# Attention heads and output mixing joined into one program block, with semaphores in place of the barrier

## The chip, the cores and the metric

The kernel runs on one core of one Trainium2 chip. The metric is the device time of one execution in microseconds (us). The core has five instruction streams that run beside each other: PE (TensorE, matmuls, with its weight loads shown as PEld), DVE (VectorE), ACT (ScalarE), POOL (GpSimd) and SP (SyncE, which here only issues DMAs). Sixteen DMA engines carry the transfers of two queues that matter here: q1, fed by SP, and q0, fed by POOL.

## The reference, cut to what matters

One layer of an encoder over 1152 tokens (1024 of a prompt and 8 x 16 of samples). The part around the change:

```python
merged = jnp.concatenate([rms_norm(og.reshape(b, t, -1)) for og in outs], axis=-1)   # three head groups
merged = (merged * g_mix_out).astype(h.dtype)
h = h + merged @ w_out                                                              # 1024 x 1024
y = hier_moe(rms_norm(h, norm_ffn).reshape(b * t, D_MODEL), w_rg, b_rg, w_re, b_re, w_eg, w_eu, w_ed)
h = h + y.reshape(b, t, D_MODEL).astype(h.dtype)
```

`outs` are the outputs of 16 attention heads. The router inside `hier_moe` takes the top group of 4 and two experts in it.

## The kernel before, in words

The program has four stages, each a block of its own: projection, heads, mixing and experts (`moe`). A block ends with a barrier over all five engines.

**Heads** (`heads`, lines 773 to 1254) goes through units of work, each one query tile of a pair of heads, software-pipelined over the engines: at step x, PE transposes the probabilities of unit x (`turn`, L1034), makes the scores of unit x + 2, transposes back the output of unit x - 2 (`back`, L1021) and multiplies with the values of unit x - 1 (`values`, L1058, or L745 and L749 for a sample unit). ACT copies and moves (`move`, L1119), DVE scans, weighs (`weigh`, L1176), copies and writes the rows (`write`). The last units are stick-breaking ones of a single head, and the very last, NU - 1, is a sample unit. Beside them the first steps of mixing are already done: `group_scale` and `norm_heads` normalise token tile 0 into `m2`, and PE transposes it (L1079) after the last values.

SP's list of heads ends with the loads for mixing: the gain `g_mix_out` (L948), the two halves of `w_out`, 2 MB each in rows of 2 KB (L950), the gain `norm_ffn` (L951), the router's weights (L952, rows of 80 bytes), its bias (L953), a column form of the gain (L954), and then a wait for all of them, `mix_loaded`, ahead of the barrier.

**Mixing** (`mixing`, lines 1280 to 1566) multiplies each of the nine token tiles with `w_out` in float32 made of parts: `split` rounds one of 8 slices (k) of a half of `w_out` on ACT (L1448), `lower_weights` subtracts that on DVE (L1509), and PE makes three matmuls of 512 columns for each k (L1374). The same is done with the transposed tile: `copy_first` (L1443) or `copies` (L1439) on ACT, and `lower` on DVE (L1518). For tile n, PE does `mix(n, 0)`, `mix(n, 1)`, transposes (L1356) and the router's logits (L1394). DVE adds the residual (`residual`, L1491), which needs both halves and the x rows that SP loaded (L1335). That sets `h_ready`, and `mix(n + 1)` waits for it.

POOL makes small tables of counts at the start of mixing, a zero tile in the memory of `z`, and issues 32 DMAs of 416 KB (L1561) that write zeros to the DRAM table `grouped`, 13 MB in all. Then it clears the semaphores of the former stages.

Memory of heads that is given back (probabilities, transposed probabilities, biases) is taken again by mixing's tiles.

Of the kernel before, what the change touches and what calls it, by code (L numbers as in the profile page):

```python
# [25 lines left out]
P = 128  # L26
# [746 lines left out]
def heads(nc, c, a, dram, merged, released, early, late, mixw):  # L773
# [6 lines left out]
    name = "heads_"  # L780
    with ExitStack() as ctx:
        sb = lambda n, s, d=F32: ctx.enter_context(nc.sbuf_tensor(name + n, s, d))
        ps = lambda n, s: ctx.enter_context(nc.psum_tensor(name + n, s, F32))
# [75 lines left out]
        mix_loaded = sem("mix_loaded")  # L859
# [24 lines left out]
        def copied(e, G):  # L884

            e.wait_ge(copied_dve if by_dve[G] else copied_act, sum(1 for F in range(G + 1) if by_dve[F] == by_dve[G]))

        with nc.Block() as block:
            @block.sync
            def _(sp):  # L890
# [58 lines left out]
                for i in two:  # L949
                    sp.dma_start(mixw["w_out"][i], wv[:, :, 512 * i:512 * i + 512]).then_inc(mix_loaded, 16)  # L950
                sp.dma_start(mixw["gff"], a["norm_ffn"].partition_broadcast(P)).then_inc(mix_loaded, 16)  # L951
                sp.dma_start(mixw["w_r"][:, :, :], a["w_router"].rearrange("(k p) n -> p k n", p=P)).then_inc(mix_loaded, 16)  # L952
                sp.dma_start(mixw["b_r"][:, :], a["b_router"].partition_broadcast(P)).then_inc(mix_loaded, 16)  # L953
                sp.dma_start(mixw["gcol"][:, :], a["norm_ffn_cols"]).then_inc(mix_loaded, 16)  # L954
                sp.wait_ge(mix_loaded, 16 * 6)

            @block.gpsimd
            def _(pool):
                for g, (h0, nh) in enumerate(pairs):
                    if not band(g):  # L960
                        continue
                    u = g % 2
                    pool.wait_ge(bias_loaded[u], expected(bias_n, g))
                    pool.memset(bias[u][HD:P, 0:nh, SEQ - PAST:SEQ - PAST + HD], NEG)
                    pool.memset(bias[u][0:HD, 0:nh, SEQ + HD:TOK], NEG).then_inc(bias_ready, 1)

            @block.tensor
            def _(pe):
# [94 lines left out]
                for x in range(NU + 2):  # L1063
# [11 lines left out]
                pe.wait_ge(opened, stuck[NU])  # L1075
                pe.wait_ge(mixw["m_normed"], 1)
                for half in two:
                    for j in range(4 * half, 4 * half + 4):
                        mm = pe.transpose(score[:, 0, P * j:P * j + P], mixw["m2"][:, P * j:P * j + P], ident[:, :])  # L1079
                    mm.then_inc(mixw["m_turned"], 1)  # L1080

            @block.scalar
            def _(act):
# [37 lines left out]
                for x in range(NU + 1):  # L1121
                    mine = [G for G in range(piece0[x], piece0[x + 1]) if not by_dve[G]] if x < NU else []
# [9 lines left out]
                    if x + 3 == NU:  # L1132
                        act.preload_act_table_set("natural_log_exp_and_others")
                    if x:
                        move(x - 1)
                    if x + 3 == NU:
                        act.wait_ge(written, NU - 4)
                        group_scale(act, c, merged[:, 0, :], mixw["m2"], mixw["sm"][:, 0, :], mixw["act_chain"], 0)
                        act.sem_inc(mixw["m_scale"], 1)

            @block.vector
            def _(dve):
# [86 lines left out]
                for x in range(NU + 2):  # L1229
# [21 lines left out]
                    if x == NU - 2:  # L1251
                        dve.wait_ge(mixw["gmo_loaded"], 16)
                        dve.wait_ge(mixw["m_scale"], 1)
                        norm_heads(dve, merged[:, 0, :], mixw["sm"][:, 0, :], mixw["gmo"], mixw["m2"]).then_inc(mixw["m_normed"], 1)

# [24 lines left out]
def mixing(nc, c, a, dram, merged, h, logits, released, mixw, x_stored, wg_raw, g_ple, counts, gate_loaded):  # L1280


    with ExitStack() as ctx:
        sb = lambda n, s, d=F32: ctx.enter_context(nc.sbuf_tensor("mix_" + n, s, d))
        ps = lambda n, s: ctx.enter_context(nc.psum_tensor("mix_" + n, s, F32))
        sem = lambda n: ctx.enter_context(nc.semaphore("mix_" + n))
        two = range(2)
        w_out, w_low, w_r, b_r, gmo, gff, gcol = (mixw[n] for n in ("w_out", "w_low", "w_r", "b_r", "gmo", "gff", "gcol"))
        w_high = [sb(f"w_high{i}", [P, KD, 512], F32R) for i in two]
        xr = sb("xr", [P, 2, D])  # L1290
        xn = sb("xn", [P, 2, D])
        rest_m2 = sb("m2", [P, D])
        m2 = [mixw["m2"]] + [rest_m2[:, :]] * (NT - 1)
        pair_mT = [sb(f"mT{u}", [P, KD, P], F32R) for u in two]
        pair_low = [sb(f"mT_low{u}", [P, KD, P], F32R) for u in two]
        mT = [mixw["mT"]] + [pair_mT[n % 2][:, :, :] for n in range(1, NT)]
        mT_low = [mixw["mT_low"]] + [pair_low[n % 2][:, :, :] for n in range(1, NT)]
        hT = sb("hT", [P, KD, P])
        sq = mixw["spare"][:, 0:D]
        sm = mixw["sm"]  # L1300
        sh = sb("sh", [P, 2])
        zeros = mixw["spare"][0:ROWS, D:D + D // 4]
        tm, tx = (mixw["score"][:, i, :].rearrange("p (u n) -> p u n", u=2) for i in two)
        om = ps("om", [P, 2, 512])
        lg = ps("lg", [P, 512])

        x_loaded = [sem(f"x_loaded{u}") for u in two]
# [1097 lines left out]
```

## Time and profile before

| what | us |
|---|---|
| median of 3 runs | 1264.49 |
| lowest and highest of the 3 | 1264.01, 1267.06 |
| the profiled execution's own time | 1266.51 |
| span of the profile (first to last instruction) | 1264.9 |
| PE busy | 1209.3 |
| heads end, mixing begins | about 665 to 670 |
| mixing ends | about 809 |

The span lies 1.6 us under the profiled execution's own time, which in turn lies 2 us over the median. Positions in the text are microseconds from the span's start.

### The profile page before, as it was taken

The page shows a single profiled execution, that of the slowest core. Times are in us where ns is not written, and L with a number is a line of the kernel's source. Part 1 is how long each engine was busy: PE and PEld are TensorE (multiplying, and loading weights), DVE is VectorE, ACT ScalarE, POOL GpSimd, SP SyncE. Part 2 cuts the span into 40 slices and gives each one's busy share as a digit, 9 for nine tenths or more (in the row PEclk, how much of TensorE's full clock was granted, in tenths as well). Part 3 has the DMA queues.
Part 4 walks back from the last instruction along what each step waited for, and adds up shares of the span by engine and source line. Part 5 has one row for each costly group of instructions (what it writes and reads, how often), then busy time and mean ns, then how long its engine had stood idle before and what let it go on. Part 6 is the DMA issues. An engine that isn't in the chain of part 4 may idle for free. (4 is left out here: it accounts for less than half of the span.)

```text
span 1264.9 us, 19690 instructions
## 1 busy us (share of the span) xinstructions
PE 1209.3 (96%) x7464; PEld 955.3 (76%) x7464; DVE 607.9 (48%) x1095; ACT 503.1 (40%) x1073; POOL 128.9 (10%) x195
## 2 busy tenths in 40 slices
PE   6999999999999999988997999799999999999998
PEld 4878888888766666655666888569999999986886
DVE  4734674310145555579985333563333343344553
ACT  5713222221255556568765344433222222213221
POOL 2000000000000000000008000031111111004321
PEclk9999999999999999989998999789999999999999
DMA  8623444514186556463458982297878888755531
GB/s 295 219 67 95 144 118 133 154 59 155 39 278 214 189 199 200 120 223 125 126 214 213 259 280 94 83 306 267 278 245 269 276 258 259 251 164 170 184 117 50
DMA packets 101980, 233.65 MB, mean 185 GB/s; under 512 B 23191, under 2 KB 50850, under 8 KB 95757
## 3 DMA queue, kind: packets, MB, share of 16 engines
q1 hardware_dynamic: 79212, 166.50, 39.2%
q0 software_dynamic: 16160, 53.50, 14.5%
q10 hardware_dynamic: 6528, 12.58, 3.8%
q8 instruction: 51, 0.84, 0.3%
q14 instruction: 29, 0.23, 0.1%
HBM read 174.70 MB, written 59.81 MB: 185 GB/s over the span
## 5 line engine op out<-in xcount | busy, mean ns | idle before, releaser
L1868 PE MATMUL moe_gu<-moe_xT,moe_room 128*128 128x208 f32 x1024 | 188.4, 343 | 0.6 <-ACT moe_xT L1996 0.6
L438 PE MATMUL zp<-w_low,x_high 128*128 128x512 f32 x432 | 175.3, 406 | 10.9 <-DVE w_low L586 8.9
L1868 PEld LDWEIGHTS moe_gu<-moe_xT,moe_room 128*128 128x128 f32 x1024 | 182.0, 192 | 2.5 <-ACT moe_xT L1996 0.9
L438 PE MATMUL zp<-w_high,x_low 128*128 128x512 f32 x432 | 171.4, 397 | 0.0
L438 PE MATMUL zp<-w_high,x_high 128*128 128x512 f32 x432 | 171.4, 397 | 0.0
L521 ACT ACTIVATE z<-zp,ssx 128x512 f32<-128x512 f32 x54 | 37.1, 687 | 203.9 <-PE zp L438 203.9
L438 PEld LDWEIGHTS zp<-w_low,x_high 128*128 128x128 f32 x432 | 81.7, 189 | 31.5 <-DVE x_low L581 11.1
L1034 PE MATMUL heads_turn<-ident,heads_prob 128*128 128x128 f32 x596 | 90.9, 283 | 7.3 <-ACT heads_probT L1112 5.5
L1087 ACT ACTIVATE heads_prob<-heads_prob,least 128x640 f32<-128x640 f32 (+7 forms) x95 | 69.2, 728 | 70.1 <-DVE least L1161 70.1
L438 PEld LDWEIGHTS zp<-w_high,x_high 128*128 128x128 f32 x432 | 81.7, 189 | 19.8
L438 PEld LDWEIGHTS zp<-w_high,x_low 128*128 128x128 f32 x432 | 81.9, 190 | 17.8
L2098 DVE COPY moe_y<-moe_yp 104x512 f32<-104x512 f32 x60 | 41.4, 691 | 106.6 <-PE moe_yp L1880 106.6
L1943 PE MATMUL moe_gu<-moe_wg_high,moe_wd_high 128*128 128x512 f32 x288 | 90.1, 393 | 0.0
L1034 PEld LDWEIGHTS heads_turn<-ident,heads_prob 128*128 128x128 f32 x596 | 65.3, 142 | 24.2 <-issue 11.8
L1112 ACT ACTIVATE heads_probT<-heads_turn 128x512 f32<-128x512 f32 (+1 forms) x131 | 68.5, 542 | 16.0 <-PE heads_turn L1034 15.5
L598 DVE TENSOR_TENSOR sq<-z 128x512 f32<-128x512 f32 (+1 forms) x36 | 18.9, 526 | 93.4 <-ACT z L521 93.4
L1943 PEld LDWEIGHTS moe_gu<-moe_wg_high,moe_wd_high 128*128 128x128 f32 x288 | 54.1, 188 | 12.5
L1188 DVE COPY heads_probT<-heads_turn 128x512 f32<-128x512 f32 (+3 forms) x51 | 31.1, 615 | 57.7 <-PE heads_turn L1034 57.5
L2004 ACT ACTIVATE moe_sig<-moe_gu 128x416 f32<-128x416 f32 x16 | 8.3, 517 | 125.7 <-PE moe_gu L1868 125.7
L1374 PE MATMUL mix_om<-w_out_low,mix_mT 128*128 128x512 f32 x128 | 51.8, 405 | 1.7 <-DVE mix_mT_low L1518 1.7
L586 DVE SCALAR_TENSOR_TENSOR w_low<-h,gmix,w_high 128x512 fp32r<-128x512 f32 x48 | 35.4, 745 | 36.7 <-ACT w_high L493 36.7
L1996 ACT ACTIVATE moe_xT<-moe_tp 128x416 f32<-128x416 f32 x64 | 29.7, 515 | 57.3 <-PE moe_tp L1862 57.3
(354 smaller groups left out, 2141.0 us busy)
## 6 DMA issues: line engine op xcount, KB each, us to landing
moe_room<-in_w_gu SPq DMA_DIRECT2D x16, 2048.0 KB, 10.2
moe_room<-in_w_ed POOLq DMA_DIRECT2D x16, 1024.0 KB, 11.5
scratch_grouped<-z POOLq DMA_DIRECT2D x32, 416.0 KB, 26.4
scratch_grouped<-moe_y SPq DMA_DIRECT2D x15, 832.0 KB
h<-in_w_in ACTq DMA_DIRECT2D x24, 512.0 KB, 5.0
scratch_qkT<-ring SPq DMA_DIRECT2D x36, 256.0 KB, 2.6
heads_ckT<-in_cache_kT SPq DMA_DIRECT2D x9, 1024.0 KB, 5.0
heads_cv<-in_cache_v SPq DMA_DIRECT2D x9, 1024.0 KB, 5.0
```

What stands on the lines that cost most here:

```text
L438: mm = pe.matmul(zp[:, U % 3, :], xs[:, k, n * P:n * P + P], ws[g % 2][:, k, :], start=(k == 0 and i == 0), stop=(k == KD - 1 and i == 2))
L521: act.activation(z[:, U % ZS, :], zp[:, U % 3, :], ACT.Copy, scale=ssx[:, 0, n:n + 1]).then_inc(group_taken, 1)
L586: dve.scalar_tensor_tensor(out=w_low[g % 2][:, k, :], in0=w_raw[:, k, :], scalar=gmix[:, k:k + 1], in1=w_high[g % 2][:, k, :].bitcast(F32) ...
L1034: mm = pe.transpose(tp[:, G % 2, P * x:P * x + P], weights_of(U, e)[:, P * b:P * b + P], ident[:, :])
L1087: act.activation(p, p, ACT.Exp, bias=least[:, U % 4, e:e + 1], scale=-1.0, accum_out=total[:, U % 4, e:e + 1]).then_inc(expd, 1)
L1112: act.activation(probT[:, U % 2, i:i + n, :].rearrange("p j n -> p (j n)"), tp[:, G % 2, 0:P * n], ACT.Copy)\
L1188: dve.tensor_copy(probT[:, U % 2, i:i + n, :].rearrange("p j n -> p (j n)"), tp[:, G % 2, 0:P * n])\
L1374: mm = pe.matmul(om[:, half, :], ms[n][:, k, :], ws[half][:, k, :], start=(k == 0 and i == 0), stop=(k == KD - 1 and i == 2))
L1868: mm = pe.matmul(gu[:, u, side, BS * f:BS * f + BS], wgu[u][:, k, DE * side + P * f:DE * side + P * f + P], xT[u][:, k, :], start=(k == 0 ...
L1943: mm = pe.matmul(gu[:, u, half, :], xs[u][:, k, :], ws[half][:, k, :], start=(k == 0 and i == 0), stop=(k == KD - 1 and i == 2))
L1996: act.activation(xT[u][:, 2 * g:2 * g + 2, :].rearrange("p j n -> p (j n)"), tp[:, g % 2, 0:2 * BS], ACT.Copy).then_inc(copied, 1)
L2098: dve.tensor_copy(to[:, t, 512 * half:512 * half + 512], yp[0:ROWS, half, :]).then_inc(y_taken, 1)
```

## The change

Mixing is no longer a block. Its five engine programs are functions (`sync`, `tensor`, `scalar_first`, `scalar`, `vector`, `gpsimd`) that heads calls at the end of its own, so that one block holds both and the barrier between them and the wait for `mix_loaded` are gone. The memory is planned as before (heads' tiles are released in the plan ahead of mixing's), and waits on counts stand where the barrier stood.

- ACT splits slices 0 to 2 of the first half before its last `move`, slice 3 after it; slices 4 to 7 wait until all values are summed; the second half waits for its own load.
- DVE lowers slices as they come, and does the last `write` and the scaling of the router's weights only after `norm_merged(1)`, ahead of `residual(0)`. The scaling waits for the four small loads.
- PE transposes tile 0 ahead of the last values.
- SP loads the x rows after the last `turn` of heads.
- POOL makes its tables once the last band bias is ready, and zeroes and issues the 32 DMAs once the last `weigh` is done. It clears the semaphores after `h_ready` is 1.

```diff
-                for i in two:
-                    sp.dma_start(mixw["w_out"][i], wv[:, :, 512 * i:512 * i + 512]).then_inc(mix_loaded, 16)
-                sp.dma_start(mixw["gff"], a["norm_ffn"].partition_broadcast(P)).then_inc(mix_loaded, 16)
-                sp.dma_start(mixw["w_r"][:, :, :], a["w_router"].rearrange("(k p) n -> p k n", p=P)).then_inc(mix_loaded, 16)
-                sp.dma_start(mixw["b_r"][:, :], a["b_router"].partition_broadcast(P)).then_inc(mix_loaded, 16)
-                sp.dma_start(mixw["gcol"][:, :], a["norm_ffn_cols"]).then_inc(mix_loaded, 16)
-                sp.wait_ge(mix_loaded, 16 * 6)
+                    sp.dma_start(mixw["w_out"][i], wv[:, :, 512 * i:512 * i + 512]).then_inc(mixw["w_out_loaded"][i], 16)
+                sp.dma_start(mixw["gff"], a["norm_ffn"].partition_broadcast(P)).then_inc(mixw["small_loaded"], 16)
+                sp.dma_start(mixw["w_r"][:, :, :], a["w_router"].rearrange("(k p) n -> p k n", p=P)).then_inc(mixw["small_loaded"], 16)
...
+                mix["sync"](sp)
...
+                pool.wait_ge(bias_ready, sum(1 for g in range(len(pairs)) if band(g)))
+                mix["gpsimd"](pool)
...
+                    if x == NU:
+                        turn_first_mixed()
                     if 0 <= x - 1 < NU:
                         values(x - 1)
...
+                    if x == NU - 1:
+                        mix["scalar_first"](act)
                     if x:
                         move(x - 1)
...
+        sp.wait_ge(*mixw["heads_turned"])
                 load(0)
                 load(1)
...
+    def scalar_first(act):
+        act.wait_ge(mixw["w_out_loaded"][0], 16)
+        split(act, 0, range(0, 3))
...
-                act.wait_ge(m_turned, 2)
+        split(act, 0, (3,))
                 copy_first(0)
-                split(0, range(0, 2))
                 copy_first(1)
-                split(0, range(2, KD))
-                split(1)
+        act.wait_ge(*mixw["heads_summed"])
+        split(act, 0, range(4, KD))
+        act.wait_ge(mixw["w_out_loaded"][1], 16)
+        split(act, 1)
...
+        def scale_router():
+            dve.wait_ge(mixw["small_loaded"], 16 * 4)
...
+        pool.wait_ge(*mixw["heads_weighed"])
                 pool.memset(zeros[:, :], 0.0).then_inc(zero_made, 1)
...
+        pool.wait_ge(h_ready, 1)
                 for s in released:
                     pool.sem_clear(s)
```

PE at the end of heads, before (`heads_out` is the output of the values, `score<-ident,w_gate_raw` the transposes of tile 0, `mix_om` the output of mixing):

```order
L1021 MATMUL heads_out<-ident,ring 128x128 [waits heads_moved]
L745 MATMUL heads_out<-ring,heads_probT 128x128 [waits heads_copied_dve,heads_cv_loaded,heads_written]
L749 MATMUL heads_out<-heads_cv0,heads_probT 32x128 x16
L1079 MATMUL score<-ident,w_gate_raw 128x128 [waits m_normed,heads_opened]
L1079 MATMUL score<-ident,w_gate_raw 128x128 x7
L888 UNCONDITIONAL_BRANCH
L1349 UNCONDITIONAL_BRANCH [waits barrier_Pool_Activation_PE_DVE_SP_release]
L1374 MATMUL mix_om<-w_out_low0,w_high 128x512 [waits mix_w_lowered,mix_m_lowered]
```

and now:

```order
L1027 MATMUL heads_out<-ident,ring 128x128 [waits heads_moved]
L1074 MATMUL score<-ident,w_gate_raw 128x128 [waits m_normed,heads_opened]
L1074 MATMUL score<-ident,w_gate_raw 128x128 x7
L745 MATMUL heads_out<-ring,heads_probT 128x128 [waits heads_copied_dve,heads_cv_loaded,heads_written]
L749 MATMUL heads_out<-heads_cv0,heads_probT 32x128 x16
L1385 MATMUL mix_om<-w_out_low0,w_high 128x512 [waits mix_w_lowered,mix_m_lowered]
```

The transposes moved ahead of the last values, and the branch and the barrier between them and the first mixing matmul are gone.

DVE from the last slices of the weights to the first residual, now (`w_out_low0` and `w_out_low1` are the lowered halves, `w_gate_raw` and `mix_m2` the normalised tiles):

```order
L1524 TENSOR_TENSOR w_out_low0<-past1,mix_w_high0 128x512 [waits mix_w_split] x5
L1524 TENSOR_TENSOR w_out_low1<-w_out1,mix_w_high1 128x512 [waits mix_w_split] x8
L768 SCALAR_TENSOR_TENSOR mix_m2<-h,merged_scales,heads_kT1 128x384 [waits m_turned,m_scale]
L768 SCALAR_TENSOR_TENSOR mix_m2<-h,merged_scales,heads_kT1 128x320 x2
L1223 TENSOR_TENSOR ring<-heads_out,parity 128x64 [waits heads_summed]
L1224 TENSOR_TENSOR ring<-heads_out,parity 128x64
L1225 TENSOR_TENSOR h<-ring 128x64 [waits heads_pick_chain]
L1529 TENSOR_TENSOR w_router<-w_router,norm_ffn_cols 128x160 [waits mix_small_loaded]
L1506 TENSOR_TENSOR h<-mix_om,mix_xr 128x1024 [waits mix_mixed,mix_x_loaded0]
```

The last write of heads and the router's scaling stand between the second tile's normalisation and the first residual, and the scaling carries the wait for the small loads.

POOL, before:

```order
L965 MEMSET heads_bias1 64x64
L888 UNCONDITIONAL_BRANCH
L1539 UNCONDITIONAL_BRANCH [waits barrier_Pool_Activation_PE_DVE_SP_gather]
L1541 IOTA mix_desc_i 128x4
...
L1557 MEMSET z 104x256
L1561 DMA scratch_grouped<-z 416x1x256 [waits mix_zero_made]
L1561 DMA scratch_grouped<-z 416x1x256 x31
```

and now:

```order
L969 MEMSET heads_bias1 64x64
L1562 IOTA mix_desc_i 128x4 [waits heads_bias_ready]
...
L1579 MEMSET z 104x256 [waits heads_weighed]
L1583 DMA scratch_grouped<-z 416x1x256 [waits mix_zero_made]
L1583 DMA scratch_grouped<-z 416x1x256 x31
```

The tables and the zeroing follow counts of heads and no longer the barrier.

## Rows read from the trace of the kernel before

**Rows 1.** The page: busy us, share and instructions of each engine.

```profile
PE 1209.3 (96%) x7464; PEld 955.3 (76%) x7464; DVE 607.9 (48%) x1095; ACT 503.1 (40%) x1073; POOL 128.9 (10%) x195
```

**Rows 2.** Stretches: length, busy PE, PEld, DVE, ACT, POOL, clock, DMA share, GB/s.

```profile
660.00:665.00 5.00, 4.53 (x65) 3.33 (x63) 3.30 (x12) 0.34 (x2) 0.00 (x0) 1.00 1.06 399
672.00:674.00 2.00, 2.00 (x6) 1.55 (x5) 2.00 (x4) 2.00 (x5) 2.00 (x3) 0.50 0.36 90
698.00:712.00 14.00, 14.00 (x76) 11.78 (x75) 5.43 (x8) 6.03 (x17) 0.00 (x0) 1.00 0.98 247
```

**Rows 3.** PE in time: start, us, line, count, idle before and its releaser.

```profile
663.85 1.09 PE L1079 MATMUL score<-ident,w_gate_raw 128*128 128x128 f32 x8
670.22 0.77 PE L1374 MATMUL mix_om<-w_out_low,w_high 128*128 128x512 f32 x1 [5.28 <-DVE w_out_low L1509]
...
683.63 1.04 PE L1356 MATMUL score<-ident,mix_m 128*128 128x128 f32 x8
686.38 0.50 PE L1374 MATMUL mix_om<-w_out_low,mix_mT 128*128 128x512 f32 x1 [1.71 <-DVE mix_mT_low L1518]
...
697.58 1.03 PE L1356 MATMUL score<-ident,h 128*128 128x128 f32 x8
```

**Rows 4.** ACT and DVE in time, from the last weigh to the first residual.

```profile
661.71 0.28 ACT L1119 ACTIVATE ring<-heads_out 128x128 f32<-128x128 f32 x1 [1.65 <-PE heads_out L1058]
673.17 4.27 ACT L1448 ACTIVATE mix_w_high<-w_out 128x512 fp32r<-128x512 f32 x8
...
656.30 0.82 DVE L1176 TENSOR_TENSOR heads_prob<-heads_prob,z 128x639 f32<-128x639 f32 x1
674.86 4.89 DVE L1509 TENSOR_TENSOR w_out_low<-w_out,mix_w_high 128x512 fp32r<-128x512 f32 x8
680.11 1.54 DVE L768 SCALAR_TENSOR_TENSOR mix_m<-h,merged_scales,heads_kT 128x384 f32<-128x384 f32 x3
683.90 1.23 DVE L1491 TENSOR_TENSOR h<-mix_om,mix_xr 128x1024 f32<-128x1024 f32 x1 [2.25 <-PE mix_om L1374]
```

**Rows 5.** SP and POOL in time: when each DMA is issued.

```profile
648.25 1.28 SPq L950 DMA_DIRECT2D w_out<-in_w_out  x1
662.79 0.43 SPq L954 DMA_DIRECT2D norm_ffn_cols<-in_norm_ffn_cols  x1
...
671.94 24.05 POOL L1561 DMA_DIRECT2D scratch_grouped<-z  x31 [0.31 <-POOL z L1557]
...
856.64 0.76 POOL L1818 DMA_DIRECT2D moe_room<-in_w_ed  x1 [10.82 <-DMA scratch_ple<-moe_late_ple]
```

**Rows 6.** DMA issues: count, KB, us to landing, one window for each.

```profile
past<-in_w_out SPq DMA_DIRECT2D x1, 2048.0 KB, 12.0
w_out<-in_w_out SPq DMA_DIRECT2D x1, 2048.0 KB, 16.6
norm_ffn_cols<-in_norm_ffn_cols SPq DMA_DIRECT2D x1, 4.0 KB, 4.8
mix_xr<-in_x SPq DMA_DIRECT2D x1, 512.0 KB, 3.6
mix_xr<-in_x SPq DMA_DIRECT2D x1, 512.0 KB, 15.7
w_gate_raw<-in_w_ple_gate SPq DMA_DIRECT2D x1, 2048.0 KB, 33.1
```

**Rows 7.** DMA queues: packets, MB, share; 725 to 730, then 860 to 863.

```profile
q0 software_dynamic: 284, 0.82, 56.4%
q1 hardware_dynamic: 396, 0.86, 44.2%
...
q1 hardware_dynamic: 66, 1.08, 84.8%
q0 software_dynamic: 39, 0.16, 12.9%
```

**Rows 8.** q1 in 665 to 666, alone on the engines.

```profile
q1 hardware_dynamic: 831, 0.07, 63.0%
```

More of the change, by code:

```diff
@@ L886, in copied @@
             e.wait_ge(copied_dve if by_dve[G] else copied_act, sum(1 for F in range(G + 1) if by_dve[F] == by_dve[G]))
+        memory.close()
+        mixw["heads_turned"], mixw["heads_summed"], mixw["heads_weighed"] = (turned, piece0[NU]), (summed, NU), (weighed, stuck[NU])
+        mix = follow(ctx)
         with nc.Block() as block:
@@ L1061, in values, with turn_first_mixed @@
                     mm.then_inc(summed, 1)
-                for x in range(NU + 2):
+                def turn_first_mixed():
+                    pe.wait_ge(opened, stuck[NU])
+                    pe.wait_ge(mixw["m_normed"], 1)
+                    for half in two:
+                        for j in range(4 * half, 4 * half + 4):
+                            mm = pe.transpose(score[:, 0, P * j:P * j + P], mixw["m2"][:, P * j:P * j + P], ident[:, :])
+                        mm.then_inc(mixw["m_turned"], 1)
+                for x in range(NU + 1):
                     if x < NU:
@@ L1071, in _ @@
                         turn(x, True)
+                    if x == NU:
+                        turn_first_mixed()
                     if 0 <= x - 1 < NU:
                         values(x - 1)
[L1075 to L1080, printed above, removed]
+                mix["tensor"](pe)
             @block.scalar
@@ L1119, in move @@
                         act.activation(oT[:, U % 2, :], op[:, U % 2, 0:P], ACT.Copy).then_inc(moved, 1)
-                for x in range(NU + 1):
-                    mine = [G for G in range(piece0[x], piece0[x + 1]) if not by_dve[G]] if x < NU else []
+                for x in range(NU):
+                    mine = [G for G in range(piece0[x], piece0[x + 1]) if not by_dve[G]]
                     while mine and mine[0] < piece0[x] + 2:
@@ L1227, in write @@
                     ins.then_inc(written, 1)
-                for x in range(NU + 2):
+                for x in range(NU + 1):
                     mine = [G for G in range(piece0[x], piece0[x + 1]) if by_dve[G]] if x < NU else []
@@ L1254, in _ @@
                         norm_heads(dve, merged[:, 0, :], mixw["sm"][:, 0, :], mixw["gmo"], mixw["m2"]).then_inc(mixw["m_normed"], 1)
+                mix["vector"](dve, lambda: write(NU - 1))
 def shift(n, u, m, d):
@@ new lines, in tensor, with split @@
+        n = NT - 1
+        mix(n, 0).then_inc(half_mixed, 1)
+        turn_rows(n - 1)
+        mix(n, 1, range(0, KD // 2))
+        route(n - 1)
+        turn_last(0)
+        mix(n, 1, range(KD // 2, KD)).then_inc(mixed, 1)
+        turn_last(1)
+        route(n)
+    def split(act, i, ks=range(KD)):
+        for k in ks:
+            act.activation(w_high[i][:, k, :], w_out[i][:, k, :], ACT.Copy).then_inc(w_split, 1)
+    def scalar_first(act):
+        act.wait_ge(mixw["w_out_loaded"][0], 16)
+        split(act, 0, range(0, 3))
@@ L2334, in program @@
             mixw |= {n: sem(n) for n in ("gmo_loaded", "act_chain", "m_scale", "m_normed", "m_turned")}
-            heads(nc, c, a, dram, merged, released, early, late, mixw)
+            mixw |= {"w_out_loaded": [sem(f"w_out_loaded{i}") for i in range(2)], "small_loaded": sem("mix_small_loaded")}
             x_stored = [sem(f"x_rows_stored{u}") for u in range(2)]
             gate_loaded = sem("gate_loaded")
-            mixing(nc, c, a, dram, merged, h, logits, released, mixw, x_stored, wg_raw, g_ple, counts, gate_loaded)
+            follow = lambda ctx: mixing(nc, ctx, c, a, dram, merged, h, logits, released, mixw, x_stored, wg_raw, g_ple, counts, gate_loaded)
+            heads(nc, c, a, dram, merged, released, early, late, mixw, follow)
             attention.close()
```

507 lines of the change are left out of this document (249 added, 258 removed).

## The prediction, made before the changed kernel was run

> **What bounds the kernel now.** I began with the page: PE is busy for 1209.3 of 1264.9 us [rows 1], so a change pays only where it gives PE something to do while it stands idle or slow. Then the table by stretches [rows 2]. In the steady part of mixing PE is busy for all of 14.00 us out of 14.00, at granted clock 1.00; no other engine is near that, so from the second tile on mixing runs at PE's pace, and whatever shifts its start shifts everything after it. The exception is the seam: about 665 to 670 PE does nothing [rows 3], and from 672 to 674 it is busy at a clock of 0.50, the lower of its two levels (1.2 GHz), after that idle stretch [rows 2]. PE in order of time gives the edges [rows 3]: the transposes of tile 0 end at 664.94, the first mixing matmul starts at 670.22 after 5.28 us idle, mix(0) ends about 683.63, and mix(1) starts at 686.38. This last number is my milestone: the kernel after gains or loses what mix(1) moves.
>
> Why the gap is 5.3 us: SP waits for the small loads ahead of the barrier. The last of them is issued at 662.79 and lands 4.8 us later, at 667.6 [rows 5, 6]; then come barrier, first copy, first lowering. The loads of w_out themselves are in time: issued at about 647.8 and 648.25, they land at 659.8 and 664.85 [rows 5, 6].
>
> **The change, compute alone.** No load is counted yet.
> - ACT does three splits ahead of its last move. Eight splits take 4.27 us [rows 4], so three take about 1.6. The first half lands at 659.8 and the move comes at 661.71 after 1.65 us idle [rows 4]: they just fit, cost 0 (up to 1 us if that load slips).
> - PE: the transposes (1.09 us) change places with the last values; a tie. DVE has lowered its first slice and the first half tile by about 664.9, so mix(0) starts at about 665.0 and not at 670.2.
> - mix(0) took 13.4 us, from 670.22 to 683.63 [rows 3]. With the clock kept it takes 16 slices at the steady pace: mix(1) is the same 48 matmuls with nothing to wait for, from 686.38 to 697.58, 11.2 us [rows 3], so mix(0) would end at 676.2. The cold clock thus cost about 2.2 us.
> - DVE then is late: the 16 lowerings, at 4.89 us for eight [rows 4], end at about 674.2; normalising tile 1 (1.54) waits for ACT's scales and ends at 676.2; the write that moved behind it and the router's scaling add 1.0, the residual 1.23, the lowering of tile 1 another 1.3. mix(1) starts at 679.8.
> - Sum: 679.8 - 686.38 = -6.6 us. The residual would start at 677.2 instead of 683.90 [rows 4].
> - Tables on POOL, made early: nothing waits for them, 0. Clearing semaphores: POOL has over 100 us for it, 0.
>
> **What the change sets loose.** This decides it. POOL's 32 zeroing DMAs (13 MB) no longer start at 671.94 but once the last weigh is done. That ends at 656.30 + 0.82 = 657.12 [rows 4]; with the zero tile made the first goes out at about 657.6, the next ones every 24.05 / 31 = 0.78 us [rows 5]. Before, all loads for mixing and the first two of x had landed by then. Now this stream meets on the 16 engines, already full (DMA share 1.06 at 399 GB/s [rows 2]), all that q1 still owes: most of the second half of w_out, the 512 KB of norm_ffn, some 1280 packets of 80 bytes and less, and the x rows. And two waits stand on these: ACT's second split on w_out's second half, DVE's residual(0) on the small loads (through the router's scaling) and on x. Behind that wait DVE's whole list is queued, and mix(1) needs both its residual and its lowering.
>
> How q1 fares beside q0. In 725 to 730, with the same zeroing deep in its queue, q1 moved 0.86 MB in 396 packets and q0 0.82 MB in 284 [rows 7]: q1 has 172 GB/s against about 400 alone. Single loads show worse, since a load waits for its slowest engine: x rows that take 3.6 us on a free machine took 15.7, and a 2 MB load of the same rows of 2 KB as w_out took 33.1 [rows 6]. A kinder row: where q1 has the backlog and q0 comes later (860 to 863), q0 got only 39 packets against 66 [rows 7], and its load had been issued at 856.64, over 3 us earlier [rows 5]; so the flood may bite only from about 661 on.
> - Second half of w_out: from 661, some 1.55 MB are left. At 172 GB/s that is 9 us, landing at 670; at the pace of the 2 MB load behind its x rows (33.1 less 15.7 gives 17.4 us for 2 MB) 13.5 us, landing at 674.5. I take 674, the nearer shape.
> - norm_ffn: 0.5 MB at 172 GB/s, 3 us: 677.
> - The small packets: alone, 831 packets went by in 1 us [rows 8], so 1.5 us for 1280. If each takes a turn against a packet of q0, at the 396 packets in 5 us of 725 to 730, they take 16 us. Nothing in the trace shows small packets in the flood. I take 8, the middle, and keep 1.5 and 16: 685.
> - x rows: 0.5 MB, 3 us, and 1 us to be reported: 689.
>
> The Trainium skill (DMA: Bandwidth & Descriptors, Queues, rings and completion order) says that each DMA engine goes round the queues that have work for it packet by packet, whatever queue came first. The near equal counts of the two queues in 725 to 730 agree with it roughly, and it speaks against starting the zeroing early; taken strictly it gives the 16 us for the small packets.
>
> **Sum.** The residual starts at 689 and not at 683.9: +5.1. PE, done with mix(0) by about 683, is idle for some 8 us before mix(1); an idle of 5.28 brought it to 0.50 and cost 2.2 us, so I add 2.3 for the longer one. Together +7.4 us. I set it against the median (the profiled run lies 2 us higher, the same shift applies to it): 1264.5 + 7.4 = 1271.9, said as 1272. After mix(1) PE's pace rules again; zeroing ends some us earlier, which nobody waits for.
>
> **The rivals.**
> 1. The loads are in time, faster. If q1's backlog goes first and small packets are nearly free, everything for residual(0) lands by 680: then the compute chain rules, -6.6, or 1258; with w_out at 670 and residual(0) at 680, about -4. For: the late start of q0 at 860. Against: 172 GB/s in 725 to 730, over many us. It would need the flood to cost less than 13 us over the 667.6 at which the last small load landed before.
> 2. Each small packet takes a turn, slower by much: the small loads end at 677 + 16 = 693, x at 697, and with the cold clock +15.4, or 1280; with w_out's half as slow as the whole 2 MB load (648.25 + 33.1 = 681, 7 us later) +22, or 1287. It decides from the point where the small loads land after 684.
> 3. Break-even: residual(0) between 680 and 688, the gap filled and the same time lost again on x. 1261 to 1268. PE then idles at 676 to 686 instead of at 665 to 670.
> 4. The change does not do what it says (the early splits delay ACT's last move by a us or more, because w_out's first half slips as well): 1 us at most, inside the range of the others.
>
> **How the numbers follow.** Faster than 1260.7 (rival 1): 0.26. Between 1260.7 and 1268.3 (rival 3, with the lower edge of the forecast): 0.24. My forecast's neighbourhood, 1268.3 to 1278: 0.28. Rival 2: 0.22. A difference of 0.3%, 3.8 us, is about the least that a measurement of this kernel can tell from no change. So faster 0.26, same 0.24, slower 0.50. The range that leaves about 2 in 10 out is 1258 to 1285.
>
> **What would show it.** The gap of PE at 665 should be gone, mix(0) should start near 665 at clock 1.00: both are sure. Then POOL's zeroing at 657.6, and the landing of w_out's second half (now 664.85): 674 for my case, under 668 for rival 1, over 680 for rival 2. DVE's router scaling waiting for a DMA, and residual(0) for a DMA on x; PE idle for 5 us or more ahead of mix(1), and its clock at 0.50 after. If residual(0) instead waits for PE only, I am wrong in the term of the flood. If mixing's later tiles take more than 14 us each, I missed contention of the x loads further on, which nothing waits for now: PE is busy 14.00 of 14.00 us there.

## The result, and the profile after

The changed kernel takes 1283.08 us (median of 4 runs, 1280.26 to 1288.64), the kernel before 1265.44 us (median of 4 runs): ratio 1.0141, 95% interval 1.0120 to 1.0162, or 17.6 us slower. The prediction said 1272, 7 us slower, with a range of 1258 to 1285. The direction holds, and so does the mechanism in kind (DVE waits for small loads that meet the early zeroing); the size is more than twice the forecast, because the small loads were priced at 8 us and took 20.8. The profiled execution of the changed kernel took 1280.26 us, with a span of 1278.3 us, 13.4 us over the span of before.

PE at the seam, kernel after; columns: start us, us, engine, line, operation, names, shapes, count, and in brackets the idle time before it and what ended it. These answer to [rows 3].

```profile
661.24 1.04 PE L1074 MATMUL score<-ident,w_gate_raw 128*128 128x128 f32 x8
662.43 1.08 PE L749 MATMUL heads_out<-heads_cv,heads_probT 128*32 128x128 f32 x32
663.65 0.50 PE L1385 MATMUL mix_om<-w_out_low,w_high 128*128 128x512 f32 x1
...
673.08 0.47 PE L1385 MATMUL mix_om<-w_out_low,w_high 128*128 128x512 f32 x1 [3.56 <-DVE w_out_low L1524]
680.29 1.04 PE L1367 MATMUL score<-ident,mix_m 128*128 128x128 f32 x8
698.95 0.80 PE L1385 MATMUL mix_om<-w_out_low,mix_mT 128*128 128x512 f32 x1 [17.62 <-DVE mix_mT_low L1538]
712.68 1.04 PE L1367 MATMUL score<-ident,h 128*128 128x128 f32 x8
```

The gap of 5.28 us at the end of heads is gone: the first mixing matmul follows the last values at once, at 663.65. But PE stops for 3.56 us in the middle of mix(0), and then for 17.62 us before mix(1), the milestone of the prediction: it starts at 698.95 and not at 686.38. The page of after has the same wait as the only large one of that line, out of 128 matmuls:

```profile
L1385 PE MATMUL mix_om<-w_out_low,mix_mT 128*128 128x512 f32 x128 | 52.8, 413 | 17.6 <-DVE mix_mT_low L1538 17.6
```

Who made PE wait stands in the time lines of ACT and DVE (answering to [rows 4]):

```profile
660.74 0.28 ACT L1129 ACTIVATE ring<-heads_out 128x128 f32<-128x128 f32 x1
671.58 4.29 ACT L1428 ACTIVATE mix_w_high<-w_out 128x512 fp32r<-128x512 f32 x8 [5.80 <-DMA w_out<-in_w_out]
...
678.53 1.54 DVE L768 SCALAR_TENSOR_TENSOR mix_m<-h,merged_scales,heads_kT 128x384 f32<-128x384 f32 x3 [1.38 <-ACTq L1438]
694.15 0.33 DVE L1529 TENSOR_TENSOR w_router<-w_router,norm_ffn_cols 128x160 f32<-128x160 f32 x1 [13.56 <-DMA norm_ffn_cols<-in_norm_ffn_cols]
696.47 1.23 DVE L1506 TENSOR_TENSOR h<-mix_om,mix_xr 128x1024 f32<-128x1024 f32 x1 [1.99 <-DMA mix_xr<-in_x]
```

Three waits for a DMA, one behind the other: ACT for w_out's second half (5.80), DVE's scaling of the router's weights for the last small load (13.56), and DVE's residual for x (1.99). DVE had done the moved write by 680.6, and did nothing from then to 694.15.

The issuing engines, in time (answering to [rows 5]):

```profile
656.84 24.05 POOL L1583 DMA_DIRECT2D scratch_grouped<-z  x31 [0.31 <-POOL z L1579]
...
647.27 1.46 SPq L954 DMA_DIRECT2D w_out<-in_w_out  x1
648.77 6.75 SPq L955 DMA_DIRECT2D heads_v<-in_norm_ffn  x1
655.56 0.52 SPq L956 DMA_DIRECT2D w_router<-in_w_router  x1
656.13 13.72 SPq L957 DMA_DIRECT2D b_router<-in_b_router  x1
669.89 3.63 SPq L958 DMA_DIRECT2D norm_ffn_cols<-in_norm_ffn_cols  x1
```

The landings (answering to [rows 6]): count, KB, us from issue to landing. `heads_v` is the memory that norm_ffn is loaded to.

```profile
w_out<-in_w_out SPq DMA_DIRECT2D x1, 2048.0 KB, 24.3
heads_v<-in_norm_ffn SPq DMA_DIRECT2D x1, 512.0 KB, 24.5
w_router<-in_w_router SPq DMA_DIRECT2D x1, 80.0 KB, 25.3
b_router<-in_b_router SPq DMA_DIRECT2D x1, 10.0 KB, 28.7
norm_ffn_cols<-in_norm_ffn_cols SPq DMA_DIRECT2D x1, 4.0 KB, 24.2
```

So w_out's second half lands at 647.27 + 24.3 = 671.6, norm_ffn at 673.3, the router's weights at 680.9, its bias at 684.8 and the last 4 KB at 694.1. The last four loads count on one semaphore, 16 steps each, and the profile gives the 16th, 32nd, 48th and 64th step to them in the order of issue: only 694.1, the last of all, is a landing beyond doubt. (Before, all six loads shared `mix_loaded`, so the same holds for the single landings that the prediction read there.) The queues in 670 to 680 (packets, MB, share of the 16 engines) show how:

```profile
q0 software_dynamic: 831, 2.44, 94.9%
q1 hardware_dynamic: 800, 0.10, 6.7%
```

Nearly equal numbers of packets, 831 and 800, but the 831 carry 2.44 MB and the 800 carry 0.10 MB. By the sizes in the trace, 594 of the 831 are packets of 4 KB (the others of 16 and 4 bytes), and 752 of the 800 are packets of 80 bytes. In [rows 8] 831 such packets of q1 went by in one microsecond, alone; beside the zeroing they need more than ten.

From here to the end the extra time stays: mixing ends at 824.43 instead of 809.23, and the experts give back 1.8 us.

**A yardstick for all that follows.** Heads end earlier or later by up to 6 us in these traces, with how often the granted clock of PE drops to 0.50 ahead of their end: never in e1 (last weigh at 653.78), in four stretches in e3 (659.72). So I cut each trace into three: the seam, from the start of the last weigh on DVE to the first matmul of mix(1) (before: 656.30 to 686.38); mixing, from there to SP's first load of the experts (809.23); the rest, from there to the end of the span. us:

| kernel | seam | mixing | rest | median of its runs, ratio to before (95%) |
|---|---|---|---|---|
| before | 30.1 | 122.9 | 455.7 | |
| after | 43.6 | 125.5 | 453.9 | 1283.1, 1.0141 (1.0120 to 1.0162) |
| e1 late zeroing | 22.6 | 123.8 | 455.8 | 1265.9, 1.0005 (0.9979 to 1.0031) |
| e7 the same, second look | 22.3 | 133.8 | 456.0 | 1271.3, one run |
| e2 small loads first | 26.3 | 125.4 | 453.5 | 1263.8, 0.9999 (0.9977 to 1.0021) |
| e8 the same, second look | 24.3 | 124.3 | 455.8 | 1263.1, one run |
| e3 router packed | 33.4 | 124.3 | 455.9 | 1269.8, 1.0039 (1.0021 to 1.0057) |
| e4 before, zeroing early | 89.7 | 122.7 | 452.6 | 1324.4, 1.0482 (1.0444 to 1.0520) |
| e5 late zeroing, small first | 22.8 | 126.0 | 456.2 | 1263.8, 0.9986 (0.9956 to 1.0016) |
| e6 before, small first | 30.6 | 122.9 | 455.6 | 1265.4, 0.9994 (0.9975 to 1.0014) |
| e10 eight zeroing DMAs early | 27.7 | 124.5 | 456.0 | 1266.9, 1.0019 (0.9999 to 1.0038) |
| e12 late zeroing, gate loads later | 22.4 | 123.0 | 453.0 | 1259.6, 0.9953 (0.9938 to 0.9968) |
| e9 late and paced zeroing | 22.4 | 122.8 | 452.8 | 1259.1, 0.9959 (0.9939 to 0.9978) |
| e11 paced, small first | 22.3 | 122.7 | 455.1 | 1256.0, 0.9932 (0.9908 to 0.9956) |

The mixing of after holds 2.5 us of cold clock (mix(1) takes 13.73 us for its 48 matmuls instead of 11.2). The last column differs by up to 3.6 us between kernels that are alike in the experts (452.6 in e4, 456.2 in e5); no experiment asks why, so no difference there is put down to an edit. All experiments compute the whole reference.

### The profile page after: what moved, and what is told of

The parts are those of the page before. It is cut to its first block and busy times, and to the rows that moved or that the text cites. A ratio compares the mean times of both kernels' runs of the same rounds, so it can differ in the third digit from the quotient of the medians.

```text
span 1278.3 us, 19677 instructions
## 1 busy us (share of the span) xinstructions
PE 1208.2 (95%) x7464; PEld 955.1 (75%) x7464; DVE 607.9 (48%) x1095; ACT 503.1 (39%) x1073; POOL 128.4 (10%) x195
## 5 line engine op out<-in xcount | busy, mean ns | idle before, releaser
L438 PEld LDWEIGHTS zp<-w_high,x_low 128*128 128x128 f32 x432 | 81.8, 189 | 17.6
L1385 PE MATMUL mix_om<-w_out_low,mix_mT 128*128 128x512 f32 x128 | 52.8, 413 | 17.6 <-DVE mix_mT_low L1538 17.6
```

The costliest lines, as they stand in the source:

```text
L438: mm = pe.matmul(zp[:, U % 3, :], xs[:, k, n * P:n * P + P], ws[g % 2][:, k, :], start=(k == 0 and i == 0), stop=(k == KD - 1 and i == 2))
L1385: mm = pe.matmul(om[:, half, :], ms[n][:, k, :], ws[half][:, k, :], start=(k == 0 and i == 0), stop=(k == KD - 1 and i == 2))
```

## The experiments

### Is it the early zeroing? e1 and e4

e1 is the changed kernel with the zeroing alone put back behind the first residual:

```diff
         pool.wait_ge(*mixw["heads_weighed"])
+        pool.wait_ge(h_ready, 1)
         pool.memset(zeros[:, :], 0.0).then_inc(zero_made, 1)
...
-        pool.wait_ge(h_ready, 1)
         for s in released:
```

> The changed kernel with one wait added: POOL makes the zero tile and issues its 32 zeroing DMAs only once the first residual is done. All else of the change stays. Theory A (the early zeroing is the whole loss): all loads land as before (last small one by about 668), PE has no gap at 665 and starts mix(1) at about 680 instead of 686.4, so 6.6 us under the kernel before, about 1259 us. Rival B (the loss comes from another part: SP's order, the moved write and scaling, the missing barrier): the router's scaling still waits for a DMA until 690 or so, and the time stays at 1275 to 1283 us. In between (1264 to 1270) both would have a share.

At the seam theory A is right to a microsecond: PE has no gap and starts mix(1) at 676.36, the seam takes 22.6 us, 7.5 under before and 21.0 under after. DVE reaches the residual at 673.89 without a wait for a DMA, and all 64 steps of the small loads' semaphore come between 662.2 and 665.2, where after they run from 666.5 to 694.1. PE and DVE in its trace:

```profile
676.36 0.50 PE L1385 MATMUL mix_om<-w_out_low,mix_mT 128*128 128x512 f32 x1 [1.71 <-DVE mix_mT_low L1538]
...
673.89 1.23 DVE L1506 TENSOR_TENSOR h<-mix_om,mix_xr 128x1024 f32<-128x1024 f32 x1 [0.19 <-PE mix_om L1385]
```

So the early zeroing is the cause of the loss at the seam. But the median, 1265.9, is that of the kernel before. The ten executions scatter from 1258.0 to 1273.9, and the trace was of the fastest. Something else takes the gain back; e7 below looks for it.

e4 is the opposite: the kernel before with the early zeroing alone. The memset and the 32 DMAs stand on POOL behind the last weigh, inside heads:

```diff
+                pool.wait_ge(weighed, stuck[NU])
+                pool.memset(zeros, 0.0).then_inc(mixw["zero_made"], 1)
...
+                for j in range(4 * LEAST_PAIRS, 4 * PAIRS):
+                    pool.dma_start(dram["grouped"]...
```

> The kernel before with one part of the change alone: POOL zeroes and issues its 32 DMAs inside heads, once the last weigh is done; barrier and wait for all six loads stay. Theory A (the early zeroing is the cause): the small loads land near 694 instead of 667.6, and the barrier, which waits for them, opens 26 us later; with a longer cold stretch of PE that makes 24 to 29 us over the kernel before, 1289 to 1294 us. Rival B (the zeroing costs little by itself; the other parts of the change lose the time): at most 5 us over, under 1271 us.

It is slower by 60 us, over twice what I expected. The small loads land as I said (bias at 687, last 4 KB at 692), but the barrier does not open then. POOL and PE in its trace:

```profile
660.01 24.05 POOL L972 DMA_DIRECT2D scratch_grouped<-z  x31 [0.31 <-POOL z L968]
725.93 0.75 POOL L972 DMA_DIRECT2D scratch_grouped<-z  x1 [41.87 <-issue]
...
732.53 0.76 PE L1381 MATMUL mix_om<-w_out_low,w_high 128*128 128x512 f32 x1 [65.40 <-DVE w_out_low L1516]
```

POOL issues 31 of the 32 DMAs in 24 us and is then held for 41.87 us before it can issue the last, and the barrier needs POOL. The same stands in the traces of before (65.95 us, to 761.94) and after (56.61, to 737.49), where nobody waits for POOL at that time. So the early zeroing alone costs time, as theory A says, but e4 loses it by another wait than the one in its theory, and its 60 us say nothing of the price of the small loads. What they show is that the early zeroing needs the barrier gone: with it kept, the loss is 60 us and not 18.

### Packets or bytes? e2, e3 and e10

e2 keeps the early zeroing and moves the three small loads (router's weights, bias, gain columns) to the head of SP's list of heads:

```diff
+                sp.dma_start(mixw["w_r"][:, :, :], a["w_router"].rearrange("(k p) n -> p k n", p=P)).then_inc(mixw["small_loaded"], 16)
+                sp.dma_start(mixw["b_r"][:, :], a["b_router"].partition_broadcast(P)).then_inc(mixw["small_loaded"], 16)
+                sp.dma_start(mixw["gcol"][:, :], a["norm_ffn_cols"]).then_inc(mixw["small_loaded"], 16)
                 for g in range(len(pairs)):
                     load_past(g)
...
```

> The changed kernel, with the early zeroing, but with the router's weights, its bias and the gain columns (1280 packets of 80 bytes and less, 0.1 MB) issued at the head of SP's list of heads, hundreds of us earlier. Turn theory (each small packet takes a turn against a 4 KB packet of the zeroing): their 20.8 us between norm_ffn's landing (673.3) and their own (694.1) go away, x rows land by about 678, DVE reaches the first residual at about 681 and mix(1) starts at about 683 to 684: 2 to 3 us under the kernel before, or 1261 to 1264 us. Byte theory (the flood takes bandwidth, the count of packets doesn't matter): 0.1 MB less to move changes under 1 us, x rows still land near 695 and the time stays within 3 us of the changed kernel, 1280 to 1283 us.

The turn theory holds: 0.1 MB less in the queue takes 17.3 us off the seam (26.3 against 43.6) and 19 us off the median (1263.8). DVE's residual starts at 681.07, without a wait for a DMA, and mix(1) at 683.53:

```profile
681.07 1.22 DVE L1506 TENSOR_TENSOR h<-mix_om,mix_xr 128x1024 f32<-128x1024 f32 x1
```

The byte theory had this at 1280 or more and falls. A second look at the same kernel (e8) gives 24.3 us at the seam, a little under the 25 to 28 I expected; its two traces have the clock under 1.00 in heads between 540 and 600 us, as those of before and after have too.

> The same kernel as the one with the small loads first, for a second look: does the seam (from the last weigh to the first matmul of mix(1), 26.3 us in the first trace against 30.1 in the kernel before) hold, and where do its executions differ (1260.5 to 1270.1)? I expect the seam at 25 to 28 us, and the difference in heads, at stretches with a granted clock under 1.00 between 540 and 600 us.

e3 leaves the order and shrinks the packets: the router's weights lie in DRAM as they will lie in memory, so that the load is 128 packets of 640 bytes.

```diff
-                sp.dma_start(mixw["w_r"][:, :, :], a["w_router"].rearrange("(k p) n -> p k n", p=P)).then_inc(mixw["small_loaded"], 16)
+                sp.dma_start(mixw["w_r"][:, :, :], a["w_router"]).then_inc(mixw["small_loaded"], 16)
...
-"w_router": np.concatenate([...], axis=1),
+"w_router": np.concatenate([...], axis=1).reshape(KD, P, NG + NE).transpose(1, 0, 2),
```

> The changed kernel, with the early zeroing and the old order of loads, but with the router's weights laid out so that their load is 128 packets of 640 bytes instead of 1024 of 80 bytes: same bytes, an eighth of the packets (384 small ones in all instead of 1280). Turn theory: the small loads end at about 678 to 682 instead of 694.1, the first residual starts at 682 to 685, mix(1) at 685 to 688, and the time is 1265 to 1269 us. Byte theory: nothing changes, 1280 to 1283 us. If SP's long issue (13.7 us for the bias load) is what counts and it doesn't depend on the packets queued ahead, it also stays above 1275.

Faster by 13 us than after (1269.8), at the seam by 10.2. That is between the two theories and nearer to the turn theory, though just outside its 1265 to 1269. The router's weights now pass quickly (issued at 660.84, landed 15.7 us later, 2.3 us behind norm_ffn instead of 7.6). But the last small load still lands 13.9 us behind norm_ffn, with 384 packets, where 1280 took 20.8. The number of packets is not all of it. The rows of its queues in 675 to 685 (packets, MB, share) say what the rest is,

```profile
q0 software_dynamic: 662, 1.94, 74.6%
q1 hardware_dynamic: 559, 0.88, 23.2%
```

and DVE in time:

```profile
688.08 0.33 DVE L1529 TENSOR_TENSOR w_router<-w_router,norm_ffn_cols 128x160 f32<-128x160 f32 x1 [2.60 <-DMA norm_ffn_cols<-in_norm_ffn_cols]
```

In 675 to 685 q1 moved 0.88 MB, nearly all of it x rows, which were issued behind the small loads; and yet the small loads were not complete before 688. My reading: a queue is spread over the 16 engines, each engine goes on to x when its own share is done, and a load counts as landed when the slowest engine has done its share. From the two traces, (20.8 - 13.9) us for 896 packets, I estimate 8 ns per packet, and some 11 us that don't depend on their number. The estimate is weak, since e3 also freed SP, which issued the last small load at 662.05 and not at 669.89.

The trace of after bears the reading out. The steps of the shared semaphore come one by one, the last sixteen of them between 685.4 and 694.1; in e1, without the flood, the last sixteen come within 1.5 us (663.7 to 665.2). And of the 1152 packets of 80 bytes, which began at 666.1, 785 pass in 669 to 679, 79 a us; from 681 on only 109 are left, and these need till 691, while the x rows behind them already move. So the turns set the pace of the bulk, and a tail of slow shares sets the landing. Why some shares are slow stays open.

e10 leaves packets and order and shortens the flood: 8 DMAs go out early, then 4 after each residual.

```diff
         for j in range(4 * LEAST_PAIRS, 4 * PAIRS):
+            late = j - 4 * LEAST_PAIRS - 8
+            if late >= 0 and late % 4 == 0:
+                pool.wait_ge(h_ready, late // 4 + 1)
             pool.dma_start(dram["grouped"]...
```

> The changed kernel, but only the first 8 of the 32 zeroing DMAs (3.4 MB) go out early; the others follow 4 after each residual. Turn theory: the small packets only take turns while q0 has work; at the 240 GB/s that q0 had in 670 to 680, 3.4 MB are gone by about 677, then the rest of the small packets passes at 831 in a us, so they end at 678 to 681 and not at 694; the seam takes 25 to 28 us (43.6 in the changed kernel, 30.1 before), the time is 1259 to 1263 us. If any early zeroing costs the same (a start-up effect, SP's blocked issue), the seam stays above 35 us and the time above 1270.

The mechanism is met: the small loads end at 679.9 (expected 678 to 681), the seam takes 27.7 us (25 to 28). The rival of SP's blocked issue falls too, since SP is held nearly as long as in after:

```profile
655.89 11.33 SPq L957 DMA_DIRECT2D b_router<-in_b_router  x1
```

The median is not met: 1266.9 against 1259 to 1263. The trace has 2.4 us less at the seam than before and 1.6 more in mixing, where mix(1) begins after an idle stretch of 5.42 us with matmuls of 0.80 us and not of 0.50; the rest of the difference lies in executions that I have no trace of.

### Were the small loads the gap of before? e6

The kernel before with the small loads first, barrier kept.

> The kernel before with one edit alone: router's weights, bias and gain columns loaded at the head of SP's list of heads; barrier kept, which now waits for w_out and norm_ffn only. The last small load landed at 667.6 and held the barrier; w_out was there at 664.85, the transposes of PE end at 664.94. Theory (the barrier's wait for the small loads was 2 to 3 us of the gap of 5.28): the gap becomes about 2.5 to 3 us, and mix(1) comes 2 to 3 us earlier, 1261 to 1262.5 us. Rival (the barrier itself and the first copy and lowering are the gap): under 0.5 us of change.

The rival has the number, 1265.4 us with a gap of 5.59 us, but not the cause: the barrier still waits for a load. Without the small loads it is norm_ffn, issued at 651.77 and landed 18.1 us later, at 669.9; the first copy starts at 670.31. So some 3.0 us of the gap (PE is idle from 666.91) are a wait for a DMA, and 2.6 are barrier, copy and lowering. On engines with no second queue the 1280 packets had cost nothing that counts. My sentence that the barrier waits for the small loads was right as a row, and wrong as a price.

### Where does late zeroing lose its gain? e7, e5, e9, e12, e11

e7 is e1 again, for a second trace.

> The same kernel as the one with the late zeroing, for a second look at its trace: its first profile (1257.96 us) lay at the low end of its ten executions (1258.0 to 1273.9), and this asks where the others lose. If the clock of TensorE drops in stretches of heads, the last weigh starts later than 653.8 and the seam still takes 22 to 23 us; if the seam itself varies, it takes more than 25 us; if mixing or the experts vary, their stretches (112.6 us from the end of mix(1) to the end of mixing, 455.8 from there to the end) get longer.

It caught a long one, 1271.3 us: seam 22.3 and rest 456.0, as in e1, but mixing 133.8 instead of 123.8. (The other 3.5 us between the two traces lie in heads.) The stretches (length, busy PE, PEld, DVE, ACT, POOL, then clock, DMA share, GB/s):

```profile
750.00:757.00 7.00, 1.24 (x10) 0.90 (x8) 2.21 (x4) 1.09 (x2) 0.00 (x0) 0.78 0.78 245
757.00:772.00 15.00, 14.41 (x55) 12.54 (x56) 6.03 (x10) 5.16 (x15) 0.00 (x0) 0.65 0.61 218
```

PE and DVE in time:

```profile
757.59 1.97 PE L1367 MATMUL score<-ident,mix_m 128*128 128x128 f32 x8 [6.35 <-DVE mix_m L768]
...
754.79 1.28 DVE L1491 SCALAR_TENSOR_TENSOR mix_xn<-h,mix_sh,heads_v 128x1024 f32<-128x1024 f32 x1 [15.38 <-DMA scratch_x_rows<-mix_xn]
```

DVE waits 15.38 us until the rows of tile 2 are stored, since tile 4's take their place; behind that wait stand the normalising of the next tile and so PE, idle for 6.35 us and then at a clock of 0.65. SP issued that store at 711.35, right behind a 2 MB load of gate weights (707.61, landed 40.0 us later); the store itself took 43.3 us. In the faster trace of e1 DVE's waits for such stores took 11.1 us in three pieces, in before 3.2 in one. Before had this collision too, with just enough slack; late zeroing lays its 13 MB fully over tiles 1 to 6 and uses it up.

e5 is late zeroing with the small loads first; its expectation was written before e7's trace was known:

> Both mends together: the changed kernel with the zeroing behind the first residual (as in the run with the late zeroing) and the small loads at the head of SP's list of heads. From the late weigh (start of the last one on DVE) to the first matmul of mix(1) the traces so far give 30.1 us for the kernel before, 43.6 for the changed one, 22.6 with late zeroing, 26.3 with the small loads first. Theory: with the zeroing gone from the seam the small loads no longer matter, so this gives 22 to 23 us, like late zeroing alone, and the profiled time is 7 us under the kernel before at equal length of heads. Whether the median shows it is open: late zeroing alone had 7.5 us less at the seam and yet a median of 1265.9 against 1264.2. If the small loads had a part there (SP's queue full), the median is now under 1262; if not, 1262 to 1266.

Seam 22.8, so the small loads don't matter once the flood is late; median 1263.8, scatter 1256.3 to 1271.5, and DVE's waits for such stores are 12.2 us in its trace. Two runs then took one of the partners of the collision away, the bulk of the zeroing (e9) or the 2 MB loads (e12); a third, e11, adds the small loads first. e9 paces the zeroing, five DMAs after each residual:

```diff
+        pool.wait_ge(h_ready, 1)
         pool.memset(zeros[:, :], 0.0).then_inc(zero_made, 1)
...
+            late = j - 4 * LEAST_PAIRS - 0
+            if late >= 0 and late % 5 == 0:
+                pool.wait_ge(h_ready, late // 5 + 1)
             pool.dma_start(dram["grouped"]...
```

> Late zeroing, and paced: POOL issues 5 of its 32 DMAs after each residual (the first five after residual(0), the last two after residual(6)) instead of all behind each other. Theory C, from the slow and the fast trace of the kernel with late zeroing: the 7.5 us won at the seam are spent in mixing, around tile 5, where DVE waits up to 15.4 us for the store of a tile's rows (scratch_x_rows), whose packets stand behind a 2 MB load and take turns with the zeroing. With 5 x 416 KB for each 14.9 us (140 GB/s) q1 keeps most of the engines, those waits go under 4 us, PE is busy through mixing, and the median shows the gain at the seam: 1257 to 1259.5 us. Rival D (the loss is not from this collision, as the clock or the experts): the median stays at 1262 to 1266, with PE busy through mixing all the same.

e12 keeps late zeroing unpaced and moves the two gate loads on SP to behind the last two x loads:

```diff
-            if n in (2, 4):
-                i = n // 2 - 1
+            if n in (5, 6):
+                i = n - 5
```

> Late zeroing, unpaced, with the two 2 MB loads of the gate weights (w_gate_raw) moved on SP from behind x loads 4 and 6 to behind x loads 7 and 8. Theory C says that the collision needs three: the stores, the 2 MB loads ahead of them in q1, and the zeroing. Without the 2 MB loads while zeroing runs, the stores land in under 20 us, DVE's wait for them is under 4 us, and the median is 1257 to 1260 us, unless the experts then wait for the gate weights (needed at about 800). If the zeroing alone suffices for the stall, it stays at 1263 to 1266.

Both reach the time: 1259.1 and 1259.6, each over 0.4% under before, with mixing at 122.8 and 123.0 us. In e9 DVE has no wait for a DMA from 700 on and PE none from mix(1) to mixing's end; POOL's groups can be seen to fit between the residuals:

```profile
681.33 4.12 POOL L1587 DMA_DIRECT2D scratch_grouped<-z  x5 [0.44 <-POOL z L1580]
694.69 3.81 POOL L1587 DMA_DIRECT2D scratch_grouped<-z  x5 [9.25 <-DVE h L1506]
...
681.70 0.50 PE L1385 MATMUL mix_om<-w_out_low,mix_mT 128*128 128x512 f32 x1 [1.71 <-DVE mix_mT_low L1538]
```

The scatter goes with the stall: e9's seven runs lie in 1257.9 to 1261.1, where e1's ten lay in 1258.0 to 1273.9. e12's ten lie in 1257.5 to 1262.8. Its DVE has no wait for a DMA in mixing either, and its slowest store lands in 16.0 us (expected under 20).

e11 is e9 with the small loads first:

> Late and paced zeroing as in the run above, and the small loads at the head of SP's list of heads: my best version. The small loads are not on the path once the zeroing is late, so the same as the paced one alone within 1 us, 1257 to 1259.5 us, 5 to 8 us under the kernel before; if Rival D holds, 1262 to 1266.

1256.0 us, 9.7 under the kernel before (ratio 0.9932, 0.9908 to 0.9956): faster than both kernels. At the seam it is like e9 (22.3 and 22.4), and the two intervals overlap, so I take the 3 us between them for nothing shown, though 1256.0 lies under the 1257 to 1259.5 that I expected.

## Why the prediction was wrong in its size, step by step

- **What bounds the kernel, and the milestone:** right. What mix(1) moved, +12.6 us in the two traces (+13.5 from the last weigh), plus the cold clock, is what mixing's end moved, +15.2. The time by medians moved 17.6; its four runs scatter over 8 us, and the profiled one is the lowest. The remaining 2 to 4 us I can't place.
- **Compute alone, -6.6 us:** right, and shown by e1 and e9, where nothing else is in the way: the seam shrinks by 7.5 and 7.7 us, and e9 is faster by 6.6. That this is the forecast's figure to the decimal is chance: in e9's trace heads take 3.0 us more than before and the rest 2.9 less. The early splits cost ACT's last move nothing (rival 4 falls).
- **Start of the flood at 657.6:** first DMA of POOL at 656.84, and its first packets at about 661, as read from the row at 860.
- **w_out's second half at 674, norm_ffn at 677:** 671.6 and 673.3. Rather kinder than forecast; ACT waited 5.80 us and PE 3.56, as a step of the same kind.
- **Small packets, 8 us:** this is the step that failed. I had worked out two ends, 1.5 us if they run as alone and 16 us if each takes a turn against a packet of the zeroing, and took the middle. They took 20.8 us, from 673.3 to 694.1 (28 us, counted from the first packet of 80 bytes at 666.1). The price per turn was right: 396 packets in 5 us in [rows 7], 79 a us, and 800 in 10 us here, 80 a us. The middle of two mechanisms is the result of neither; the row at hand that showed two queues with backlog side by side [rows 7] spoke for the upper end. And even this end was short by 5 us: it had no term for the tail of slow shares, which the trace of after shows and whose cause is open.
- **x rows and the cold clock:** x landed 2.4 us after the small loads (forecast 4), the clock cost 2.5 us (2.3).
- **The forecast's sum again with 20.8 in the place of 8,** from norm_ffn's own 673.3: small loads 694.1, x 697 to 698, residual +14, with the clock +16. That is rival 2, which said small loads 693, x 697 and +15.4 with its chance of 0.22, and it is what happened in kind. Its 693 for the small loads against 694.1 is partly luck: norm_ffn came 4 us earlier than it assumed, and the small packets took 5 us longer.
- **The page of the Trainium skill** (DMA: Bandwidth & Descriptors, Queues, rings and completion order) says that an engine takes the queues with work in turn, packet by packet. The 831 and 800 packets in 670 to 680 agree with it, but loosely: 594 of the 831 are of 4 KB, the page's packet holds several descriptors, and no run here shows how it relates to what the profile counts. The 284 and 396 of [rows 7], which I called near equal, agree still less. I cited the page and then halved what it gave.
- **"Zeroing ends some us earlier, which nobody waits for":** right for the changed kernel, whose DVE never waits for the stores of rows from 700 to 800. The contention that I named as a way to be wrong came only in the kernels with late zeroing.

## What to carry to other kernels

When a bulk stream on one DMA queue may start earlier, list what the other queue still owes at that moment, in packets and not in bytes: small loads that cost nothing on free engines here cost 17 us of the seam beside 4 KB packets (after against e2). Issue them well ahead (17.3 us less at the seam), lay them out in longer rows (10.2 us less), or hold the stream back and pace it by the consumer's own semaphore (here five DMAs a tile), which removed both the stall at the seam and the one in mixing. And where two bounds are two mechanisms, choose one and give the other its chance; don't take the middle.

## What the runs showed of the hardware that I had not expected

- POOL could have 31 of these 416 KB DMAs issued and was held at the 32nd for 41.87 (e4) to 71.54 us (e7) where all go out behind each other. Paced in e9, it was held there for 5.13 us. What frees it was not tested. An engine that has to reach a barrier behind such a stream is late by that time (e4, 60 us).
- SP's issue of the 10 KB bias load took 13.72 us beside the early zeroing and 5.48 before (11.33 in e10); the x loads behind it on SP went out at 673.56 and not at 661 as in e1. In e3, with an eighth of the packets ahead of it, the same issue took 0.60 us. All fit one reading, that SP's issue waits on the packets still queued ahead of it; it was not tested alone.
- A 4 KB load, issued at 669.89, took 24.2 us to land, where it took 4.8 alone [rows 6].
- Two executions of one kernel (e1 and e7) differed by 10 us in one stage through a single wait whose slack was nearly used up; a trace of a fast one alone would have hidden it.
